# Fox attention heads: outputs gated two at a time out of PSUM, the first pair prepared beside the gate product, and no joins around the heads

## The reference

```python
k = rms_norm(split_heads(k), k_gain)            # shared keys
F = cumsum(log_sigmoid(f_logit + f_bias))       # per head and token
qg = h @ w_qg; q, gate = qg[..., :D], qg[..., D:]
q = rms_norm(split_heads(q), q_gain)
s = q @ k.T * 64**-0.5 + F[t] - F[s]            # only keys s <= t
p = softmax(s); o = p @ v
y = (o * sigmoid(gate)) @ w_o
```

## Time and profile before

| | |
|---|---|
| median of 3 runs | 3405.2 us (3399.24 to 3406.45) |
| the profiled execution | 3386.05 us, span 3384.7 us |
| PE busy | 3063.1 us, 90% |
| DVE, ACT, POOL busy | 60%, 33%, 3% |
| mean granted PE clock | 0.936 |
| chain that ended last | PE 69%, DVE 19%, ACT 5%, DMA 5% |

### The profile page before, as it was taken

The page is one execution under the profiler, slowest core; times in us unless marked ns, Lnnn a source line. Parts: engine busy times, 40 slices in busy tenths (PEclk is TensorE's granted clock), DMA queues, the critical chain, the costliest instruction groups (busy, mean ns, idle before and its releaser), DMA issues.

```text
span 3384.7 us, 45906 instructions
## 1 busy us (share of the span) xinstructions
PE 3063.1 (90%) x19574; PEld 2499.1 (74%) x19577; DVE 2033.0 (60%) x3132; ACT 1105.0 (33%) x1685; POOL 91.1 (3%) x101
## 2 busy tenths in 40 slices
PE   6998899998988998986988778799999998799999
PEld 5876787886766787873757777678887787678887
DVE  5856895876576885866436777644444254545353
ACT  2334332223263431322324333242123343442121
POOL 0000000000000000000001211000000001100000
PEclk8998999998998998997988888799999997999999
DMA  8751454544512444540310000222332220023232
GB/s 238 176 181 43 159 181 149 177 161 150 180 47 82 167 131 163 185 143 14 108 24 8 11 12 7 73 86 95 100 100 76 88 99 13 7 75 97 91 99 87
DMA packets 236401, 345.56 MB, mean 102 GB/s; under 512 B 19605, under 2 KB 121949, under 8 KB 236197
## 3 DMA queue, kind: packets, MB, share of 16 engines
q1 hardware_dynamic: 217780, 327.27, 30.1%
q10 hardware_dynamic: 18416, 15.36, 1.7%
HBM read 340.45 MB, written 2.15 MB: 101 GB/s over the span
## 4 chain that ended last, share of the span: by engine, by line
PE 69%; DVE 19%; ACT 5%; DMA 5%; issue 1%; SPq 0%; DVEq 0%; ACTq 0%
PE bank L141 67%; DVE w_tiles L150 3%; DVE w_low L150 3%; DVE ada_acc L162 2%; PE bank L144 2%; ACT w_high L147 1%; ACT stage L147 1%; DMA weight_ring<-in_f_w_down 1%; DMA first_ada<-in_w_ada 1%; DVE x_natural L150 1%; DVE u_low L150 1%; DMA weight_ring<-in_f_w_up 1%; DMA weight_ring<-in_d_w_in 1%; DVE x_natural L162 1%; DVE stage L150 1%
## 5 line engine op out<-in xcount | busy, mean ns | idle before, releaser
L150 DVE TENSOR_TENSOR w_low<-weight_ring,w_high 128x2048 fp32r<-128x2048 f32 (+2 forms) x212 | 463.9, 2189 | 609.2 <-ACT w_high L147 609.2
L147 ACT ACTIVATE w_high<-weight_ring 128x2048 fp32r<-128x2048 f32 (+2 forms) x212 | 388.1, 1831 | 767.6 <-DMA weight_ring<-in_mlp_down 171.3
L141 PE MATMUL bank<-u_high,w_high 128*128 128x512 f32 x1472 | 583.7, 397 | 14.4 <-DVE w_low L150 5.4
L141 PE MATMUL bank<-u_low,w_high 128*128 128x512 f32 x1472 | 576.7, 392 | 0.0
L141 PE MATMUL bank<-u_high,w_low 128*128 128x512 f32 x1472 | 576.5, 392 | 0.0
L141 PE MATMUL bank<-w_high,u_high 128*128 128x512 f32 x896 | 354.8, 396 | 11.4 <-DVE u_low L150 6.5
L141 PE MATMUL bank<-w_low,u_high 128*128 128x512 f32 x896 | 351.0, 392 | 0.0
L141 PE MATMUL bank<-w_high,u_low 128*128 128x512 f32 x896 | 350.9, 392 | 0.0
L141 PEld LDWEIGHTS bank<-u_high,w_high 128*128 128x128 f32 x1472 | 278.7, 189 | 84.6 <-DVE u_low L150 17.0
L141 PEld LDWEIGHTS bank<-u_high,w_low 128*128 128x128 f32 x1472 | 278.5, 189 | 59.4
L141 PEld LDWEIGHTS bank<-u_low,w_high 128*128 128x128 f32 x1472 | 278.8, 189 | 56.3
(11 more groups left out here) (388 smaller groups left out, 4337.4 us busy)
## 6 DMA issues: line engine op xcount, KB each, us to landing
ada_ring<-in_mod_w SPq DMA_DIRECT2D x48, 1024.0 KB, 7.4
weight_ring<-in_f_w_up SPq DMA_DIRECT2D x44, 1024.0 KB, 5.1
ada_ring<-in_w_ada SPq DMA_DIRECT2D x40, 1024.0 KB, 7.3
weight_ring<-in_mlp_up SPq DMA_DIRECT2D x32, 1024.0 KB, 5.4
weight_ring<-in_mlp_down SPq DMA_DIRECT2D x32, 1024.0 KB, 5.0
weight_ring<-in_f_w_down SPq DMA_DIRECT2D x24, 768.0 KB, 4.7
weight_ring<-in_m_w_in SPq DMA_DIRECT2D x16, 1024.0 KB, 9.9
weight_ring<-in_d_w_in SPq DMA_DIRECT2D x12, 1024.0 KB, 5.2
```

Source lines behind the costliest of these rows:

```text
L141: return self.e.matmul(out, l, r, start=start, stop=stop, skip_group_check=True)
L147: return self.e.activation(out, in_, f, **kw) if self.live else QUIET
L150: return self.e.tensor_tensor(out, a, b, op) if self.live else QUIET
```

## The change

- The output of a unit is no longer a `tensor_scalar` each. Both heads of a pair sum into bank 5 side by side (`hs(hh)` columns), and when the second is done DVE takes both out with two `scalar_tensor_tensor`, each bank times reciprocal times gate. Only the first head's sum waits for outputs, those of the pair of units before.
- The gate multiplies after the heads (three on DVE, one on POOL) go, and so do the three joins. PE waits for the last output instead; POOL's first keys wait for the inverse norms.
- DVE's four preparations, both query passes and both `x_fh` passes of the first pair are put ahead of `dve_beside(v, "x_gate")`. For that the constants and `x_fh` get other places in SBUF (over the gate weights and sums used up by then), and the first pair is transposed into banks 3 and 2 right behind the gate product; DVE, not ACT, copies the first `x_qt`. The block of keep-warm matmuls is 8 instead of 16 and 4.
- The DVE passes for the next pair are spread: one query pass each at `g % 8` of 0 and 1, `x_fh` at 3 and 5 (`dve_x_forget`) instead of both behind the key copy at 6.
- Waits for banks go through `self.free`.

```diff
--- before.py
+++ after.py
@@ -394,15 +394,18 @@
         self.x_xn = [self.x_gate[:, t, :] for t in range(3)] + [self.x_q[:, 1, :]]
         self.x_f, self.x_fb, self.x_sm = take("x_f", [16, 2, S]), take("x_fb", [16, 1]), take("x_sm", [P, 192])
         self.x_gain, self.x_f2 = take("x_gain", [P, 2, HD]), take("x_cum_parts", [P, S])
+        spent = ar.top
         self.x_gw = self.gate_tiles("x", 16, 16)
         self.x_cum, self.x_cum_high = take("x_cum", [16, S]), take("x_cum_high", [16, S], F32R)
         ar.top = base
         self.x_qn, self.x_kn = take("x_qn", [P, TT, P]), take("x_kn", [P, TT, P])
         self.x_qt, self.x_kt = take("x_qt", [P, 2, S]), take("x_kt", [P, 2, S])
-        self.x_p, self.x_pt, self.x_pick = take("x_p", [P, 3, S]), take("x_pt", [P, 2, S]), take("x_pick", [P, 16])
+        self.x_p, self.x_pt = take("x_p", [P, 3, S]), take("x_pt", [P, 2, S])
+        assert ar.top <= lin
+        ar.top = spent
         self.x_fh, self.x_ones = take("x_fh", [P, 2, 2, S], F32R), take("x_ones", [P, P], F32R)
         self.x_ident, self.x_causal = take("x_ident", [P, P], F32R), take("x_causal", [P, P], F32R)
-        assert ar.top <= lin
+        self.x_pick = take("x_pick", [P, 16])
         ar.top = lin + 4 * 4 * 4096
         self.x_gb = self.x_k[:, 0, :]
         ar.top = lin + 19 * 4096
@@ -2636,10 +2639,8 @@
         turn(range(4, KT))
         self.pe_linear_t(pe, "x_q", self.u, self.A, u="x q")
         self.pe_linear_t(pe, "x_gate", self.u, self.A)
-        self.join(pe, self.T, "x heads start")
         self.pe_fox_heads(pe)
-        self.join(pe, self.T, "x heads end")
-        self.join(pe, self.T, "x gated")
+        pe.wait_ge(self.V, "x out", X_UNITS - 1)
         self.pe_turn(pe, "x o u", lambda t: self.x_q[:, t, :])
         self.pe_linear_t(pe, "x_out", self.u, self.V, u="x o u")
 
@@ -2670,11 +2671,9 @@
         self.act_evict(a, "x_q", self.x_q, ACT.Copy)
         self.act_inv_sqrt(a, "x heads", self.x_sm[:, 0:128])
         self.act_evict(a, "x_gate", self.x_gate, ACT.Sigmoid)
-        self.join(a, self.A, "x heads start")
         self.act_fox_heads(a)
-        self.join(a, self.A, "x heads end")
+        a.wait_ge(self.G, "x kn", 7)
         self.act_gate_load(a, "x", self.x_gb)
-        self.join(a, self.A, "x gated")
         self.act_turn(a, "x o u", None, None)
         self.act_residual(a, "x_out", lambda t: self.act_normed_behind(a, "g1", "x_out", lambda t: self.g[1]["xn"][:, t, :], t),
                           lambda t: self.act_squares(a, "x_out", 0, t))
@@ -2705,24 +2704,25 @@
                 v.tensor_reduce(sm[:, i * 8 + 16 * t:i * 8 + 16 * t + 8], sq.rearrange("p (g d) -> p g d", d=HD), ALU.add).then_inc(
                     *self.V.up())
         self.dve_inv_sqrt(v, "x heads", sm[:, 0:128], 1.0 / HD, NORM_EPS)
+        for j in range(2):
+            self.dve_x_queries(v, 0, j)
+        v.tensor_copy(self.x_ones[:], self.ones[:]).then_inc(*self.V.up())
+        v.tensor_copy(self.x_ident[:], self.ident).then_inc(*self.V.up())
+        v.tensor_copy(self.x_causal[:], self.causal_q).then_inc(*self.V.up())
+        v.tensor_tensor(self.x_pick[:], self.ident[:, 0:16], self.ident[:, 32:48], ALU.add).then_inc(*self.V.up())
+        v.wait_ge(self.V)
+        for hh in range(2):
+            self.dve_x_forget(v, 0, hh)
         self.dve_beside(v, "x_gate")
-        self.join(v, self.V, "x heads start")
         self.dve_fox_heads(v)
-        self.join(v, self.V, "x heads end")
-        for t in (1, 2, 3):
-            v.tensor_tensor(self.x_q[:, t, :], self.x_q[:, t, :], self.x_gate[:, t, :], ALU.mult).then_inc(*self.V.up())
-        self.join(v, self.V, "x gated")
         self.dve_turn(v, "x o u")
         self.dve_modulate(v, "g1", MOD_W["mod_w1"] + 24, self.cols["norm_mlp_g_2"][:, 8:16])
         self.dve_residual(v, "x_out", "x", self.x_gb, 1.0, follow=lambda t: self.dve_rms_behind(v, "g1", "x_out", t))
 
     def pool_fox(self, g):
-        self.join(g, self.G, "x heads start")
+        g.wait_ge(self.V, "rsqrt", "x heads")
         for p in range(8):
             self.pool_x_keys(g, p)
-        self.join(g, self.G, "x heads end")
-        g.tensor_tensor(self.x_q[:, 0, :], self.x_q[:, 0, :], self.x_gate[:, 0, :], ALU.mult).then_inc(*self.G.up())
-        self.join(g, self.G, "x gated")
 
     def dve_forget(self, v):
         lf, t0 = self.x_f[:, 0, :], self.x_f[:, 1, :]
@@ -2752,10 +2752,10 @@
         return g // 8, g % 2, g % 8 // 2
 
     def pe_fox_heads(self, pe):
-        self.pe_keep(pe, self.lin["x_gate"].group(0), 16)
-        self.pe_x_turned(pe, 0, 0, 7)
-        self.pe_x_turned(pe, 0, 1, 6)
-        self.pe_keep(pe, 5, 4)
+        spare = self.lin["x_gate"].group(0)
+        self.pe_x_turned(pe, 0, 0, spare + 3)
+        self.pe_x_turned(pe, 0, 1, spare + 2)
+        self.pe_keep(pe, spare, 8)
         for g in range(X_UNITS + 3):
             if g < X_UNITS:
                 if g % 2 == 0:
@@ -2772,27 +2772,27 @@
     def pe_x_turned(self, pe, p, keys, b):
         if keys:
             pe.wait_ge(self.G, "x kn", p)
-            if b == 7:
-                pe.wait_ge(self.A, "x qt", p)
         else:
             pe.wait_ge(self.V, "x qn", p)
-            if p:
-                pe.wait_ge(self.V, "x kt", p - 1)
+        if b in self.free:
+            pe.wait_ge(*self.free[b])
         for t in range(TT):
             m = pe.transpose(self.bank[b][:, t * P:(t + 1) * P], (self.x_kn if keys else self.x_qn)[:, t, :], self.ident)
         m.then_inc(*self.T.up("x kturned" if keys else "x qturned", p))
-        self.free[b] = (self.V, "x kt", p) if keys else (self.A, "x qt", p)
+        self.free[b] = (self.V, "x kt", p) if keys else (self.V, "x qt", p) if p == 0 else (self.A, "x qt", p)
 
     def x_score_bank(self, g):
         return (0, 1, 2, 6)[g % 4]
 
     def pe_x_scores(self, pe, g):
         if g % 8 == 0:
-            pe.wait_ge(self.A, "x qt", g // 8)
+            pe.wait_ge(self.A if g else self.V, "x qt", g // 8)
+            pe.wait_ge(self.V, "x kt", g // 8)
             pe.wait_ge(self.V, "x fh", g // 8)
         for u in (g, g + 1):
-            if u >= 4:
-                pe.wait_ge(self.A, "x exp", u - 4)
+            b = self.x_score_bank(u)
+            if b in self.free:
+                pe.wait_ge(*self.free[b])
         for u in (g, g + 1):
             p, hh, i = self.x_unit(u)
             rows, n, bank = slice(HD * hh, HD * hh + HD), (i + 1) * P, self.bank[self.x_score_bank(u)]
@@ -2805,28 +2805,29 @@
             self.free[self.x_score_bank(u)] = (self.A, "x exp", u)
 
     def pe_x_ptr(self, pe, g):
-        i, bank = self.x_unit(g)[2], 3 + g % 2
+        i, bank_at = self.x_unit(g)[2], 3 + g % 2
+        bank = self.bank[bank_at]
         pe.wait_ge(self.A, "x exp", g)
-        if g >= 2:
-            pe.wait_ge(self.A, "x pt", g - 2)
+        if bank_at in self.free:
+            pe.wait_ge(*self.free[bank_at])
         for j in range(i + 1):
-            m = pe.transpose(self.bank[bank][:, j * P:(j + 1) * P], self.x_p[:, g % 3, j * P:(j + 1) * P], self.ident)
+            m = pe.transpose(bank[:, j * P:(j + 1) * P], self.x_p[:, g % 3, j * P:(j + 1) * P], self.ident)
         m.then_inc(*self.T.up("x pturned", g))
-        self.free[bank] = (self.A, "x pt", g)
+        self.free[bank_at] = (self.A, "x pt", g)
 
     def pe_x_mixed(self, pe, g):
         p, hh, i = self.x_unit(g)
         pe.wait_ge(self.A, "x pt", g)
-        if g >= 1:
-            pe.wait_ge(self.V, "x out", g - 1)
+        if hh == 0 and 5 in self.free:
+            pe.wait_ge(*self.free[5])
         for j in range(i + 1):
-            m = pe.matmul(self.bank[5][:, 0:HD], self.x_pt[:, g % 2, j * P:(j + 1) * P],
+            m = pe.matmul(self.bank[5][:, hs(hh)], self.x_pt[:, g % 2, j * P:(j + 1) * P],
                           self.x_v[:, j, p * P + hh * HD:p * P + hh * HD + HD], j == 0, j == i)
         m.then_inc(*self.T.up("x mixed", g))
-        self.free[5] = (self.V, "x out", g)
+        if hh:
+            self.free[5] = (self.V, "x out", g)
 
     def act_fox_heads(self, a):
-        self.act_x_taken(a, 0)
         for g in range(X_UNITS + 2):
             if g < X_UNITS:
                 n = (self.x_unit(g)[2] + 1) * P
@@ -2856,15 +2857,24 @@
         rr = r.rearrange("p (t h) -> p t h", t=TT)[:, :, 2 * p:2 * p + 2].unsqueeze(3)
         return rr.to_broadcast([P, TT, 2, HD])
 
-    def dve_x_queries(self, v, p):
-        if p:
-            v.wait_ge(self.T, "x qturned", p - 1)
+    def dve_x_queries(self, v, p, j):
         cut = lambda x: x.rearrange("p t (h d) -> p t h d", h=2)
         flat = self.x_qn[:].rearrange("p t (h d) -> p (t h) d", h=2)
-        v.tensor_tensor(cut(self.x_qn[:]), cut(self.x_q[:, :, p * P:(p + 1) * P]), self.x_pair(p, self.x_sm[:, 0:64]), ALU.mult).then_inc(
-            *self.V.up())
-        v.wait_ge(self.V)
```

(56 more changed lines are left out.)

## The result

The changed kernel takes a median of 3357.49 us (3355.25 to 3359.14, 4 runs) against 3402.22 (3393.35 to 3406.45, 4 runs) for the kernel before: a ratio of 0.9871, 95% interval 0.9849 to 0.9894. That is 44.7 us, where 19.1 were forecast.

The account below looks back on a forecast made before the run. It took PE, in places DVE, to carry the heads, with low clock costing up to 6.2 us a pair. Terms 6.3 + 4.2 + 1.5 - 1.4 + 8.5 = 19.1 us, from 3405.2 to 3386.1 us; range 3368 to 3397.

Parts of the forecast that it names:

- The sum: Whole diff: start, key copies, query passes, paired outputs and end together give 19.1 us, clock in the heads as before.
- the query saving: Heads at `g % 8 == 0`: second query pass moves away, net 0.5 us in three full-clock pairs, 1.5 us.
- Start: Before the heads: first-pair preparation moves beside the gate product, first score comes earlier, gain 6.3 us (5.9 to 6.8).
- The split: Weight split behind the moved DVE work: ends later but is covered by 6 us, cost zero; uncovered 6.3 us.
- Rival (4): Start: no gain since the weight split comes late, 6 us back, 3392; 10% together with the POOL rival.
- Pair at full clock: Heads: a sign that the forecast holds, a full-clock pair of 15.6 to 15.7 us against 16.58 before.
- Outputs two at a time: Heads: even sum waits 0.2 us longer for two outputs, once a pair, loss 1.4 us in seven.
- End: Behind the heads: no gate pass or joins, transposes start earlier and at full clock, gain 8.5 us.
- rival (3): Heads: POOL holds DVE at the moved passes and outputs are at their worst, 3392; 10% together with the late-split rival.
- the clock in the heads as it was: Heads: low-clock pairs stay as before the change, so the terms count as summed; 50% (3381 to 3391).
- another number of low pairs than three: Heads: a sign that would prove the prediction wrong, if windows after the change show it.
- Rival (1): Heads: the full clock holds, three low pairs regained give up to 19 us more, 3368; chance 23%.

Follow-up runs that it names:

- e10: Kernel before plus six keep-warm matmuls on PE at each of seven key copies, ahead of the waiting sum: 3364.95 us, ratio 0.9903.
- e6: Changed kernel plus two useless DVE passes of `x_fh` size behind each key copy: 3391.04 us, ratio 0.9986.
- e7: Changed kernel with both query passes together at `g % 8 == 0`, `x_fh` still spread: 3359.94 us, ratio 0.9894.
- e3: Kernel before with only the spread of DVE's query and `x_fh` passes: 3368.55 us, ratio 0.9901.
- e8: Changed kernel with outputs one by one, still gated as they leave PSUM: 3349.56 us, ratio 0.9856.
- e4: Kernel before with only gated outputs two at a time, no gate pass and no joins behind the heads: 3393.93 us, ratio 0.9986.
- e9: Changed kernel plus one useless DVE pass behind each key copy: 3370.23 us, ratio 0.9921.
- e1: Kernel before once more, with no edit: 3403.28 us, ratio 0.9994.
- e12: Changed kernel with outputs one by one, measured a second time on another chip: 3350.08 us, ratio 0.9856.
- e11: Changed kernel again, with no edit, on another chip: 3349.15 us, ratio 0.9861.
- e2: Kernel before with only the start changed, first pair prepared beside the gate product: 3395.64 us, ratio 0.9979.
- e5: Changed kernel without the spread, query and `x_fh` passes back in their old places: 3378.20 us, ratio 0.9945.

## Why the prediction went wrong, step by step

**The sum was right.** With all pairs at 1.00 on both sides, the diff is worth e10's stretch less that of after: 153.1 - 133.4 = 19.7 us. I had 19.1. It counted the query saving in the three full pairs only; with all six full it would have been 20.6, so it was 0.9 too high on its own terms. By the medians on one chip it is 3364.95 - 3349.15 = 15.8, and 19.7 is within what these two intervals allow.

- Start: 9.17 - 2.92 = 6.25 us (predicted 6.3). The split was covered, as argued; the moved work is 4.6 us, where I had allowed 7.3. Rival (4) did not come.
- Pair at full clock: 16.58 to 15.77, 0.81 (predicted 15.6 to 15.7). The parts: the `x_fh` passes at the key copy 0.80 (16.57 in e6 against 15.77; predicted 0.8), the query place 0.72 (e7; predicted 0.7). The spread alone gives 1.39 a pair (e3). Outputs two at a time cost 0.58 a pair (15.77 against e8's 15.19), or 0.70 beside the old order (e4). My sum has 0.2 for each of key copy, query place and one even sum, 0.6 a pair, which is what it is. What I did not see is that single outputs, gated just the same, would have avoided that loss (e8).
- End: 34.34 in e10 to 25.66, 8.7 us. That includes the last key copy, so the forecast to hold against it is 8.5 and 0.6, 9.1. Transposes at 1.00, 3.71 us (predicted 3.7).
- A `scalar_tensor_tensor` out of PSUM: 280 ns (predicted 284).
- POOL at the moved pass, rival (3): it slows DVE, and nothing waits for that. At 2896.85 the `x_fh` pass took 0.78 us instead of the 0.48 of e9's useless pass, beside POOL's of 1.05 from 2896.30. The prediction cited the Trainium skill (SBUF — State Buffer, "Who interferes with whom"); this row shows such a delay, at less than the whole of POOL's instruction. The row of 1.23 us that the prediction set beside that sentence is a `tensor_tensor`; by the same section such an operation has no two-port mode and contends with GpSimd through its second input in SBUF, so the row bears on the exclusion and not on that mode.

**The step that failed is "the clock in the heads as it was".** It was put at no change, and there are no low pairs after the change instead of three; "another number of low pairs than three" was among the signs of being wrong. I saw that the lower level costs up to 6.2 us a pair, wrote that "the diff does not set it directly", and gave the case that it holds 23%. Against it I put that the same gap came in later pairs with no fall. That was the wrong inference. e1 shows that a stand of this length brings the clock down in some pairs of some executions; three pairs without a fall say that it is not certain, not that the stand is innocent. By PE's wait at the key copy the runs order themselves:

| PE waits at the key copy | runs | granted clock of the six pairs behind the first |
|---|---|---|
| 0.65 to 0.66 us | e3, e8, e12 | 1.00 in all |
| 0.84 to 0.85 | after, e7, e11 | 1.00 in all |
| 1.23 to 1.25 | e9 | 1.00, 0.90, 0.63, 0.82, 1.00, 0.90 |
| 1.44 to 1.46 | before, e1, e2 | 0.63 to 0.90 in three, three and five of six |
| 1.63 to 1.64 | e4, e5, e6 | 0.63 to 0.76 in four, six and five of six |
| 1.44, filled | e10 | 1.00 in all |

The mean clocks are of one profiled execution each. The last row makes it a cause: the wait for the output is the same, only PE is busy in it. The two `x_fh` passes behind the copy made the stand long; the diff shortened it from 1.44 to 0.84. Filling it is worth 31 to 33 us in e10 (26 to 40 by the interval), more than all that the sum counted. On that chip the 46.9 us between the kernel before and the changed one (3396.09 - 3349.15) are these 31.1 and the 15.8 that e10 leaves. The first set of the changed kernel, 3357.49, is 8 above e11's, no more than the other stages vary.

The Trainium skill (TensorE: Matmul & The Clock Gate, "A second HAM failure mode: psum-queue depth-cycling") describes a kernel in which short stands between groups of matmuls make the clock go back and forth and cost throughput. The runs here agree: in the profiled executions the stretch lost 17.0 us to it (before) and 9.9 (e1), and by the medians filling the stands gave back 31.

**The second step that failed is the size.** Rival (1) was bounded at 3368 by the three low pairs of one profile. That execution was a mild one: 170.1 - 153.1 = 17.0 us lost in the stretch, where filling the stands gave 31 by the medians. What the average execution loses there is not measured directly. An estimate: the rest of the span, outside the stretch, is 3218.5 us on average over the 14 profiles, which leaves 176 and 182 us of the medians 3396.09 and 3402.22 for the stretch, 23 and 29 more than 153.1. The 19 us between the profiled execution and the median, of which I wrote that "no row tells where it sits", were low clock somewhere in the kernel: its time follows its mean clock over 62 executions. That they sat in the heads is not shown for all of them. e1's profiled execution took 8.3 us longer than that of before, though its stretch was 7.2 shorter; its extra time lies ahead of the heads, 10 us of it in the window of the RWKV-7 block above. Had I added the 16 to 19 to rival (1), it would have read 3350, close to e11, but by counting all of it for the heads.

What stays open: why of two equal stands one brings the clock down and the other does not (e6's two windows), and what in the RWKV-7 block and ahead of it decides how long its clock is low; no run filled or shortened a stand there. How long a stand at the query passes would have to be to do harm was not tried. Whether single outputs are faster in total was not settled; by e11 and e12 the difference is under what such a measurement tells.

## What to carry to other kernels

Where a profile shows stretches at the lower clock, look at the longest stand of PE ahead of each, take the executions' spread and the distance from profile to median as a sign of such loss, somewhere in the kernel, and test the stand by filling it with matmuls of no use before anything is reordered: six at each of seven key copies gave 31 us here. A vector operation of half a microsecond between a copy and the output that PE waits for can cost six to seven times its length that way (5.6 us of them cost 34 to 39 in e6, 2.8 cost 20 in e9); put it where DVE is idle. A stand that did no harm in one pair of one profile has not been shown harmless.
